# Squares for every second down tile from the 52nd on, and their turns one place later in VectorE's order

## The reference

```python
def peer_ffn(h, w_query, sub_keys1, sub_keys2, expert_down, expert_up):
    ...
    top_v, pos = lax.top_k(cand, TOPK)
    expert_idx = jnp.take_along_axis(cand_idx, pos, axis=-1)
    gates = jax.nn.softmax(top_v, axis=-1).astype(h.dtype)
    ...
    def one_block(args):
        h_blk, idx_blk, g_blk = args
        u = jnp.take(expert_down, idx_blk, axis=0)
        act = jax.nn.gelu(jnp.einsum('bpd,bphkd->bphk', h_blk, u))
        vv = jnp.take(expert_up, idx_blk, axis=0)
        return jnp.einsum('bphk,bphkd->bpd', g_blk * act, vv)
```

## Time and profile before

| | us |
|---|---|
| three executions | 1538.61, 1539.0, 1540.46 |
| median | 1539.0 |
| the profiled execution | 1540.89 |
| its span, first to last instruction | 1539.6 |
| 1 busy in the span: PE | 1500.0 (97%) |
| DVE | 1081.1 (70%) |
| ACT | 657.8 (43%) |
| POOL | 434.8 (28%) |

### The profile page before, as it was taken

The page is one execution under the profiler, slowest core; times in us unless marked ns, Lnnn a source line. Parts: engine busy times, 40 slices in busy tenths (PEclk is TensorE's granted clock), DMA queues, the critical chain, the costliest instruction groups (busy, mean ns, idle before and its releaser), DMA issues.

```text
span 1539.6 us, 25208 instructions
## 1 busy us (share of the span) xinstructions
PE 1500.0 (97%) x9851; PEld 1264.4 (82%) x9851; DVE 1081.1 (70%) x1895; ACT 657.8 (43%) x982; POOL 434.8 (28%) x285
## 2 busy tenths in 40 slices
PE   8999999999999888999999999999999999999998
PEld 5777878875755577599999999999999888888887
DVE  5788788664765754667988875656556777777776
ACT  4456453643321511343444443334334445455453
POOL 0000000000010200028888888888884000000000
PEclk9999999999999989999999999999999999999999
DMA  9777574357555920356767666666664777777776
GB/s 343 270 244 247 193 259 138 137 191 250 193 197 177 397 88 22 137 165 186 144 138 147 142 139 158 144 164 144 159 152 109 239 240 240 238 240 240 239 241 232
DMA packets 179850, 297.24 MB, mean 193 GB/s; under 512 B 51434, under 2 KB 88066, under 8 KB 179732
## 3 DMA queue, kind: packets, MB, share of 16 engines
q1 hardware_dynamic: 133072, 277.08, 53.8%
q0 software_dynamic: 39296, 8.55, 8.0%
q10 hardware_dynamic: 7364, 9.99, 2.0%
HBM read 276.54 MB, written 19.03 MB: 192 GB/s over the span
## 4 chain that ended last, share of the span: by engine, by line
PE 87%; DVE 5%; ACT 3%; issue 2%; DMA 2%; ACTq 1%; DVEq 0%
PE bank L577 22%; PE bank L579 22%; PE bank L581 21%; PE bank L1189 6%; PE bank L572 5%; PE bank L1120 1%; ACTq L2101 1%; PE bank L1136 1%; PE bank L549 1%; PE bank L927 1%; DVE gt L1299 1%; PE bank L939 1%; PE bank L938 1%; DVE w_low L1318 1%; PE bank L629 1%
## 5 line engine op out<-in xcount | busy, mean ns | idle before, releaser
L2653 POOL DMA_INDIRECT c_dram<-gates,places x256 | 412.4, 1611 | 149.6 <-issue 77.7
L577 PE MATMUL bank<-hT_high,dT_high 128*128 128x256 f32 x1024 | 296.0, 289 | 0.0
L579 PE MATMUL bank<-hT_low,dT_high 128*128 128x256 f32 x1024 | 289.0, 282 | 0.0
L581 PE MATMUL bank<-hT_high,dT_low 128*128 128x256 f32 x1024 | 285.6, 279 | 0.0
L2558 ACT CAST up_high<-slot 128x1024 fp32r<-128x1024 f32 x128 | 134.3, 1049 | 157.8 <-DMA slot<-in_expert_up_dram 157.8
L577 PE MATMUL bank<-up_high,A_high 128*128 128x512 f32 x512 | 200.0, 391 | 1.0 <-DVE A_low L1318 1.0
L579 PE MATMUL bank<-up_low,A_high 128*128 128x512 f32 x512 | 200.7, 392 | 0.0
L581 PE MATMUL bank<-up_high,A_low 128*128 128x512 f32 x512 | 199.2, 389 | 0.0
L577 PEld LDWEIGHTS bank<-hT_high,dT_high 128*128 128x128 f32 x1024 | 192.8, 188 | 4.6 <-issue 0.2
L581 PEld LDWEIGHTS bank<-hT_high,dT_low 128*128 128x128 f32 x1024 | 193.5, 189 | 0.0
L579 PEld LDWEIGHTS bank<-hT_low,dT_high 128*128 128x128 f32 x1024 | 192.6, 188 | 0.0
(11 more groups left out here) (454 smaller groups left out, 2545.9 us busy)
## 6 DMA issues: line engine op xcount, KB each, us to landing
slot<-in_expert_up_dram SPq DMA_DIRECT2D x128, 512.0 KB, 3.5
slot<-in_expert_down_dram SPq DMA_DIRECT2D x97, 512.0 KB, 3.7
slot<-in_w_in_dram SPq DMA_DIRECT2D x41, 1024.0 KB, 5.2
P<-in_w_ada_dram SPq DMA_DIRECT2D x16, 1024.0 KB, 7.9
c_dram<-zeros SPq DMA_DIRECT2D x1, 16384.0 KB, 50.9
slot<-c_dram SPq DMA_DIRECT2D x128, 128.0 KB, 3.4
slot<-in_expert_down_dram SPq DMA_DIRECT2D x124, 128.0 KB, 2.8
slot<-in_w_in_dram SPq DMA_DIRECT2D x6, 2048.0 KB, 8.9
```

The source lines that it names most:

```text
L577: pe.matmul(o, lhsT=lhs_high.bitcast(F32R), rhs=rhs_high.bitcast(F32R), start=start, stop=False, skip_group_check=True)
L579: pe.matmul(o, lhsT=lhs_high.bitcast(F32R), rhs=rhs.bitcast(F32R), start=False, stop=False, skip_group_check=True)
L581: return pe.matmul(o, lhsT=lhs.bitcast(F32R), rhs=rhs_high.bitcast(F32R), start=False, stop=stop, skip_group_check=True)
L2653: g.indirect_dma_start(C_dram, bass.IndirectOffsetOnAxis(ap=places[:, x, k:k + 1], axis=0), gates[:, x, k:k + 1], None, compute_op=ALU.add ...
```

## The change

Two places. The list of squared tiles was 51, 53, 56, 58, 61 and so on, two of every five, 31 in all; it becomes every odd number from 51 to 127, 39 in all. And DVE does the square turn of tile n+1 behind the low part of n, where it did that of n+2.

```diff
-    SQUARED = [n for n in range(N_KEYS) if n > 49 and n % 5 in (1, 3)]
+    SQUARED = [n for n in range(N_KEYS) if n > 49 and n % 2 == 1]
...
-        if n + 2 in squared_at:
-            v_square_turn(n + 2)
+        if n + 1 in squared_at:
+            v_square_turn(n + 1)
```

## The result

The changed kernel takes 1565.16 us (median of four executions, 1563.51 to 1568.13) against 1539.09 for the kernel before beside it: a ratio of 1.017, 95% interval 1.0152 to 1.0188. It is slower by 26 us; the profiled execution took 1565.88, its span is 1563.8.

A forecast was written before the change was run, and what follows sets the result against it. PE (97% busy) and the scatter chain were taken to end the down stage nearly together, scatters then setting the end. 1540.9 + 25.4 (later up start) + 1.7 (clock) = 1568.0, median 1.9 lower: 1566; range 1543 to 1573 us.

The forecast's parts named there:

- PE's share: Down stage, 78 tiles: eight turns go, 3.285 us a tile for 3.46, down products ending 13.7 us earlier.
- The beat: Down stage: low parts of squares every 6.57 us, each making one scatter in three take 2.55 us instead of 1.56.
- the edge: Lead over a scatter with which a DVE instruction wins: between 0.03 and 0.08 us; the forecast lead was 0.10.
- What does not delay a scatter: Down stage: transposes, and low parts read from a PSUM bank, overlap scatters of 1.55 us without effect.
- The count: Scatters from the 126th on: 37 pairs, 243.1 us, 111 scatters; the last of all ends at 1202.1 us, 28.6 later.
- The hand-over: Down to up stage: 3.67 us from last scatter to DVE's first multiplication, 2.70 more to PE's start at 1208.5.
- The clock: Start of the up stage, after PE's long pause: half speed costs between nothing and 3.4 us, 1.7 taken.
- The scatter wins: Down stage: the scatter comes first at each second meeting, seven scatters in 13.14 us, 1529.5 us in all; chance 0.09.
- The pace stays: Down stage: PE keeps its stall, beat 6.80 us, seven scatters in 13.6 us, 1535.7 us in all; chance 0.09.
- No meeting counts: Down stage: all scatters come 1.86 us apart, 1527.4 us in all; chance 0.02.

The follow-up runs named there:

- last 16 left out: The changed kernel without the last 16 of the 256 scatters: 1534.85 us, 0.9972 of the kernel before.
- one transpose twice: The changed kernel with the first of eight transposes of each PE-turned tile from the 53rd on done twice: 1535.96 us, 0.9983 of the kernel before.
- the list alone: The kernel before with the list of 39 odd tiles but the old order of square turns: 1539.79 us, ratio 1.0009.
- squares turned into PSUM: The changed kernel with DVE's square turns written into two PSUM banks instead of SBUF, rounding and low part in halves: 1526.77 us, 0.9922 of the kernel before.
- order alone: The kernel before with its 31 squared tiles but the square turn of n+1 behind the low part of n: 1559.23 us, ratio 1.0135.
- one transpose four times: The changed kernel with the first transpose of each PE-turned tile from the 53rd on done four times: 1543.74 us, 1.0026 of the kernel before.

## Why the prediction was right

Predicted 1566 us, measured 1565.2, inside the range, slower as forecast. In the profiled executions 1568.0 was forecast and 1565.9 came; this one reached the 125th scatter 2.2 us earlier than that of the kernel before (917.64 for 919.85), before the change has any part in it, and that is about the whole difference.

- *PE's share* held. Turns come without their stall, the pair takes 6.57 us, no wait of PE is left in the down stage, and the down products end at 1166.6 (39.34 us ahead of 1205.96), in an execution in which PE was already 2.4 us ahead when it began the down product of tile 50 (912.10 for 914.53). Less that, 13.7 us earlier, as worked out.
- *The beat* held, and so did the edge on which it hangs: due scatters 0.09 to 0.14 us behind the low part, 2.51 to 2.57 us long, 37 of them behind the one of 1.90, one in three. The forecast stood 0.02 us from the edge as it was then known. Over all runs the smallest lead with which a low part won is 0.07 us (last 16 left out, 962.80 against 962.87, a scatter of 2.58), the largest with which one lost is 0.02 (one transpose twice, 1108.93 against 1108.95, a scatter of 1.56).
- *What does not delay a scatter* was right, but rows 4 and 5, to which it is put down, show no scatter that starts inside a transpose. The trace of the kernel before has one well inside the transpose of 1004.18, and 43 more, all of 1.55 or 1.56 us. Inside low parts read from PSUM 14 start, but 0.11 to 0.15 us before their end, all of 1.55 or 1.56 too; with one transpose twice 18 start 0.58 to 0.60 us before it, all of 1.55. The one inside the transpose:

```profile
1004.46 1.56 POOL L2653 DMA_INDIRECT c_dram<-gates,places  x1 [0.30 <-issue]
```

- *The count*: 28.6 us more for the scatters by the sum, 28.5 in the trace.
- *The hand-over*: 3.67 and 2.70 us were taken over from before, 3.68 and 2.61 came.
- *The clock*: 1.7 us was chosen between 0 and 3.4, and 1.7 came (4.33 less 2.62), of which 1.3 are left at the end of the span. This was the weakest term; that it was right is luck, since no such pause was in the trace and the middle of two bounds was taken. The upper bound is the stretch of 6.80 us at a granted clock of 0.50, ahead of which PE waits 2.7 us at the longest (480 to 545 us); what a pause of 39 us brings, no trace of the kernel before shows. In the changed kernel the clock was 0.50 from 1205.9 to 1209.5 us, for 3.6 us of up products.
- *The rivals.* The scatter wins: excluded in the changed kernel, but 0.11 us more of PE work a pair made it so, at 1536 us. The pace stays: excluded here; its pace is what the list alone does, seven scatters in 13.52 us for 13.6 worked out, at 1539.8 us where 1535.7 was worked out. No meeting counts: excluded by the long scatters, and seen as a number, 1526.8 us for 1527.4 worked out, once the squares were turned into PSUM. The runs show that a low part with both inputs in SBUF holds up the scatter that starts inside it (2.51 to 2.57 us for 1.55 in the changed kernel), that a low part that starts with a scatter, within 0.02 us, is held up a little (1.24 to 1.27 us for 1.22, one transpose twice), and that no scatter is held up when one input is in PSUM (at most 1.58, squares turned into PSUM); by which part of the chip, they don't show.

## What to carry to other kernels

A stage in which the bottleneck engine never waits can still end together with a chain on another engine: before making the first faster, read where each chain ends at the hand-over, and what sets the second one's pace. Where one engine can hold up another and each repeats with a fixed period, they can lock, each meeting setting up the next, as 37 low parts 6.57 us apart did here with every third scatter: the two periods then decide how many meetings cost something and how much, and not the number of instructions that could meet. Here 0.11 us more a pair made the changed kernel 29 us faster, and 0.20 us less (6.77 us in the list alone, 6.57 in the changed kernel) made it 25 us slower. The remedy is not to tune the period but to take away the meeting, here by keeping one operand in PSUM (1526.77 us, no scatter over 1.58).

## What the runs showed of the hardware

For these low parts and scatters the delay is lopsided. A low part with both inputs in SBUF that starts 0.09 us ahead of a scatter (order alone, 1012.77) makes it take 2.57 us for 1.55: DVE ends 1.14 us after the scatter's start, and the scatter ends 1.43 us after that, as behind every low part of a squared tile that met one in these traces, within 0.02. In these traces a scatter held up a low part only around its own start: a low part 0.01 us behind it (one transpose twice, 1002.16) takes 1.25 us for 1.22, a loss of 0.03, and one 0.09 us behind it (the list alone, 1006.99) loses nothing and the scatter neither, though both then run side by side for over a microsecond. And a pause of PE of 3.08 us (one transpose four times) was already followed by an up product of 0.77 us, as one of 39.34 us was (the changed kernel), while behind 1.76 us (the list alone) it took 0.47. With one transpose four times the granted clock was 0.59 on average from 1182.1 to 1185.7 us, in the changed kernel 0.50 from 1205.9 to 1209.5, with the list alone 1.00 from 1177.1 to 1180.7.
